# Dealing a background stream of matmul pieces to ten expert passes by their work, on one Trainium2 core

## The chip, the cores and the metric

The kernel runs on one core of a Trainium2 chip. Its time is the device time of one execution, in microseconds (us). The kernel before was run three times: 1731.17 us in the median (1726.09 to 1734.52). Names of engines: PE is TensorE (PEld its weight loads), DVE VectorE, ACT ScalarE, POOL GpSimd, SP SyncE. The queues of SP and ACT issue the loads spoken of here, on one set of 16 DMA engines.

## What is computed

Two blocks follow one another on 256 tokens of width 1024, all in float32. The first ends in a mixture of experts; the second starts with an mLSTM and pooling mixer that needs the states of a context of another 256 tokens. Cut to what matters:

```python
def first_block(x, c, ctx, ...):
    ...                                  # token mixer, residual
    x = x + gt2 * hier_moe(modulate(rms_norm(x, norm2_g), sh2, sc2), ...)
    return rms_norm(x, final_norm_g)

def hier_moe(h, wg, bg, we, be, w_gate, w_up, w_down):   # 4 groups x 8 experts, top 2
    ...                                  # router: combine[token, group, expert]
    for gi in range(N_GROUPS):
        hid = (silu(einsum('td,edf->tef', t, w_gate[gi]))
               * einsum('td,edf->tef', t, w_up[gi]) * combine[:, gi, :, None])
        out = out + einsum('tef,efd->td', hid, w_down[gi])

def mlstm_pool_mixer(hx, hc, ...):       # second block, layer 0
    uc = hc @ w_in                       # the context's half: independent of x
    hc_f, st_f = mlstm_chunkwise(...)    # 4 heads, forward and backward
    yc = mlstm_pool_output(...)          # gates, head norm, pooling, w_out
# then ctx = ctx + gate_c * rmsnorm(yc, g_post[0]), and the norm of layer 1
```

The context's half of that mixer, up to and with its two norms, does not need x. The kernel computes it while the weights of the experts arrive.

## The kernel before, in words

Each expert has three matrices of 2.1 MB. All 32 experts are loaded and used, whatever the router chose; tokens are gathered to the experts' slots by matmuls with a 0/1 matrix. The experts are done in ten passes (`PASSES`): passes 0 to 5 take four experts each (32 slots an expert), passes 6 to 9 take two (64 slots each). A pass has six steps on PE, each with one half of a matrix of each expert of the pass: gate, gate, up, up (`project`), down, down (`down`). A half is 128 x 2048 words, and the halves lie in eight slots (`half_slot`, `NHALF`). SP issues the loads of a step as soon as the step that used those slots is over (`sparse_sync`, waits on `step_used`). So in a pass of four experts two steps are loaded ahead, in a pass of two experts four. PE waits on `step_in` at the start of each step.

Between `project` and `down` a pass has on PE the gather of the next pass's tokens (`gather`), then the transposes of the hidden rows, which wait for DVE's product of both projections (`hid_out`). Behind the down projection ACT and DVE copy one half of the result each, ACT issues its store to `expert_rows` in HBM, and after the last pass POOL gathers from there the two rows of each token (`rows_pool`). ACT and DVE scale and add these at the very end of the stage, behind the rest of the context stream (`finish(body)`).

The context stream is written as generators, one each for PE, ACT and DVE (`body_pe`, `body_act`, `body_dve`), with the same number of pieces. `start(body)` takes 4 pieces; `fill(body, p, i)` takes the pieces that a table gives for pass p at place i of nine; `finish(body)` takes what is left. On PE the places 0, 1 and 2 are behind the first three halves of the projections, place 3 is behind the gather, place 4 behind the transposes, places 5 and 6 behind the two down halves, 7 and 8 at the pass's end. ACT and DVE have their places between the same dependencies. A piece on PE is mostly half of a PSUM bank's matmuls of one weight chunk: 8 matmuls 128 x 256 or 4 of 128 x 512. The pieces stand in this order: keys and values of the first two heads, gate columns, memory of head 0 and 1 (nine small pieces each, with ACT and DVE between them), output gates O and Z, queries, keys, values and memory of the other two heads, O and Z again, pool inputs PU, four pool pieces, pool gates PG, sixteen output pieces (`out_pe`, lines 1532 and 1537), and two norms of two pieces each (`norm_steps_pe`: a sum of squares, line 1253, and its spread over the partitions, line 1263). The context's weights come by ACT's queue in four slots of their own (`f_load`, line 1379), two tiles ahead.

Lines of the profile: 2346 projections, 2363 down, 2332 gather, 2379 transposes, 2218 weight loads, 1417 and 1432 pieces of context projections, 1445 and 1451 gate columns, 1462 to 1474 the start of a head's memory, 1485 to 1496 its other pieces, 2300 to 2313 the row numbers on DVE in pass 0, 2416 and 2419 ACT's copy and store, 2321 POOL's gathers, 2425 and 2476 the join of the rows, 1967 and 1973 the residual of the first norm, 424, 402 and 414 a norm of another stage with the same shapes.

Of the kernel before, what the change touches and what calls it, by code (L numbers as in the profile page):

```python
# [227 lines left out]
def build(nc, d, out):  # L228
    ctx = ExitStack()
    with ctx:  # L230
        def sb(name, shape, dt=F32):
            return ctx.enter_context(nc.sbuf_tensor(name, shape, dt))
# [27 lines left out]
        work = sb("work", [P, WORK])  # L260
# [1023 lines left out]
        NPOOL = len(POOLS)  # L1284
# [883 lines left out]
        PASSES = [(N_WIDE + 4 * i, 4) for i in range((NX - N_WIDE) // 4)] + [(2 * i, 2) for i in range(N_WIDE // 2)]  # L2168
# [50 lines left out]

        step_of = [n for n in range(6 * NPASS) for _ in range(PASSES[n // 6][1])]  # L2220

        FILL_FOUR, FILL_TWO = (2, 2, 2, 2, 2, 2, 2, 1, 1), (0, 0, 0, 1, 0, 1, 0, 0, 0)

        def fill(body, p, i):

            for _ in range((FILL_FOUR if PASSES[p][1] == 4 else FILL_TWO)[i]):
                next(body, None)

        def start(body):
# [94 lines left out]
        def sparse_pe(pe, body):  # L2324
# [12 lines left out]
            def project(p, b, n, at):  # L2337

                experts = PASSES[p][1]
                w = P // experts  # L2340
                for half in range(2):
                    pe.wait_ge(step_in[(n + half) % 4], filled_to[n + half])
                    for k in range(4 * half, 4 * half + 4):
                        for e in range(experts):
                            rows = slice(e * w, (e + 1) * w)
                            mm = nc.tensor.matmul(bank[b][rows, :], gath[:, k, rows], half_slot[(load_at[n + half] + e) % NHALF][:, (k % 4) * 512:(k % 4 + 1) * 512],  # L2346
                                                  start=(k == 0), stop=(k == DT - 1), skip_group_check=True)
                    mm.then_inc(step_used, 1)
                    if at + half < 3:
                        fill(body, p, at + half)  # L2350

            def down(p, n):

                experts = PASSES[p][1]
                w = P // experts
                for half in range(2):
                    pe.wait_ge(step_in[(n + half) % 4], filled_to[n + half])
                    for f in range(2 * half, 2 * half + 2):
                        for side in range(2):
                            for e in range(experts):  # L2360
                                rows = slice(e * w, (e + 1) * w)
                                at = (f % 2) * D + side * 512
                                mm = nc.tensor.matmul(bank[2 + side][rows, :], phid_t[:, f, rows], half_slot[(load_at[n + half] + e) % NHALF][:, at:at + 512],  # L2363
                                                      start=(f == 0), stop=(f == 3), skip_group_check=True)
                    mm.then_inc(step_used, 1)
                    fill(body, p, 5 + half)
# [3 lines left out]
            for p in range(NPASS):  # L2370
                pe.wait_ge(gath_out, 2 * p + 2)
                project(p, 0, 6 * p, 0)
                project(p, 1, 6 * p + 2, 2)
                if p < NPASS - 1:
                    gather(p + 1)
                fill(body, p, 3)
                pe.wait_ge(hid_out, p + 1)
                for f in range(4):
                    mm = nc.tensor.transpose(bank[0][:, f * P:(f + 1) * P], phid[:, f * P:(f + 1) * P], ident[:])
                mm.then_inc(phid_mm, 1)  # L2380
                fill(body, p, 4)
                if p < NPASS - 1:
                    pe.wait_ge(gath_out, 2 * p + 4)
                pe.wait_ge(phid_t_out, p + 1)
                down(p, 6 * p + 4)
                fill(body, p, 7)
                fill(body, p, 8)
# [796 lines left out]
```

## Time and profile before

| | us |
|---|---|
| median of three runs | 1731.17 |
| the profiled execution | 1726.63 |
| its span, first to last instruction | 1724.8 |
| first projection matmul of pass 0 | 540.0 |
| first of pass 6 | 995.3 |
| end of the last down projection | 1130.2 |
| last instruction of the stage (DVE) | 1166.3 |

On the page PE is busy for 90% of the span, DVE for 28%, ACT for 20%, and HBM is read at 230 GB/s on average. The 40 slices are 43 us long; slices 13 to 26 hold the expert stage, in which the DMA row reads 8 or 9 tenths and PE's 8 or 9. A busy share of an engine in a stretch is its busy time by the stretch's length. The DMA share is the mean of the 16 engines; a stretch in which they never pause reads 1.01.

### The profile page before, as it was taken

Reading aid. Unit: us, or ns where it says so; the run is one execution under the profiler, and the core shown is the slowest. Engines: PE = TensorE matmul, PEld = TensorE weight load, DVE = VectorE, ACT = ScalarE, POOL = GpSimd, SP = SyncE. Lnnn points to the kernel's source line nnn. Section 1 sums busy time; section 2 is a strip of 40 time slices with the busy share of each in tenths; the row PEclk is TensorE's granted clock in tenths of the full one; section 3 lists DMA queues with packets and bytes.
Section 4 is the critical chain, followed back from the end, with each engine's and each line's share of the span. In section 5 each row is a group of like instructions: output and inputs, shape, how many; then the busy total and the mean of one; then the engine's idle time right before and its main releaser. Section 6 shows DMA issues by size and latency. Waiting matters only on the chain.

```text
span 1724.8 us, 22009 instructions
## 1 busy us (share of the span) xinstructions
PE 1557.5 (90%) x9293; PEld 1069.7 (62%) x9293; DVE 487.9 (28%) x1221; ACT 340.9 (20%) x706; POOL 4.1 (0%) x8
## 2 busy tenths in 40 slices
PE   6999979899979879988998999976889989999997
PEld 3655678778865433643364754555676776888666
DVE  2200164451134321222114100024343322022481
ACT  2310150212021112011210000023112032021461
POOL 0000000000000000000000000000000000000000
PEclk8999996799979889999999999986999999999998
DMA  9989530122148998999999999941313223323100
GB/s 378 421 350 377 201 130 1 49 101 98 49 189 339 379 410 361 412 395 408 416 395 418 402 407 423 374 185 38 146 49 139 105 98 126 135 93 147 49 2 25
DMA packets 54303, 397.57 MB, mean 230 GB/s; under 512 B 6359, under 2 KB 13688, under 8 KB 16440
## 3 DMA queue, kind: packets, MB, share of 16 engines
q1 hardware_dynamic: 40384, 341.85, 49.4%
q10 hardware_dynamic: 13240, 52.16, 7.6%
q0 software_dynamic: 576, 2.10, 0.4%
q8 instruction: 75, 1.23, 0.3%
q14 instruction: 28, 0.23, 0.0%
HBM read 389.80 MB, written 6.29 MB: 230 GB/s over the span
## 4 chain that ended last, share of the span: by engine, by line
PE 77%; DMA 9%; DVE 5%; ACT 4%; issue 2%; SPq 1%; PEld 1%; ACTq 0%; PEldq 0%; DVEq 0%
PE bank L680 15%; PE bank L1417 12%; PE bank L1432 8%; PE bank L2346 6%; DMA work<-in_moe_w_up 4%; PE bank L2363 4%; PE bank L1532 3%; PE bank L1537 3%; PE bank L525 2%; PE bank L2332 2%; DMA work<-in_moe_w_gate 2%; PE bank L711 2%; DMA work<-in_ada_w 2%; PE bank L1140 2%; PE bank L1128 2%
## 5 line engine op out<-in xcount | busy, mean ns | idle before, releaser
L680 PE MATMUL bank<-H,ring 128*128 128x256 f32 (+1 forms) x960 | 244.7, 413 | 6.1 <-ACT work L1057 4.0
L680 PEld LDWEIGHTS bank<-H,ring 128*128 128x128 f32 x960 | 183.0, 192 | 59.7 <-issue 34.2
L2346 PE MATMUL bank<-ring,work 128*32 128x512 f32 (+1 forms) x768 | 137.4, 626 | 17.3 <-DMA work<-in_moe_w_gate 6.3
L1417 PE MATMUL bank<-H,work 128*128 128x256 f32 x512 | 114.1, 381 | 0.1
L1417 PE MATMUL bank<-H,ring 128*128 128x256 f32 x512 | 112.9, 381 | 0.0
L1417 PEld LDWEIGHTS bank<-H,work 128*128 128x128 f32 x512 | 96.0, 190 | 18.7 <-issue 6.2
L1417 PEld LDWEIGHTS bank<-H,ring 128*128 128x128 f32 x512 | 98.1, 192 | 13.6
L2346 PEld LDWEIGHTS bank<-ring,work 128*32 128x32 f32 (+1 forms) x768 | 36.5, 121 | 105.2 <-issue 83.4
L1432 PE MATMUL bank<-work,H 128*128 128x512 f32 x192 | 85.2, 596 | 0.0
L1432 PE MATMUL bank<-ring,H 128*128 128x512 f32 x192 | 83.0, 592 | 0.0
L2363 PE MATMUL bank<-ring,work 128*32 128x512 f32 (+1 forms) x384 | 67.5, 618 | 2.8 <-issue 2.2
L2346 PE MATMUL bank<-work 128*32 128x512 f32 (+1 forms) x256 | 65.4, 659 | 3.6 <-DMA work<-in_moe_w_up 3.6
L1432 PEld LDWEIGHTS bank<-work,H 128*128 128x128 f32 x192 | 35.7, 190 | 47.0 <-issue 46.9
L1432 PEld LDWEIGHTS bank<-ring,H 128*128 128x128 f32 x192 | 36.5, 190 | 44.2 <-issue 44.0
L525 PEld LDWEIGHTS bank<-work,csil 128*32 128x32 f32 x1536 | 42.5, 114 | 12.8 <-issue 11.0
L525 PE MATMUL bank<-work,csil 128*32 128x128 f32 x1536 | 49.3, 283 | 0.5 <-DMA work<-in_ada_w 0.5
L2332 PEld LDWEIGHTS bank<-work 128*128 128x128 f32 x320 | 38.1, 199 | 10.9 <-issue 7.5
L2363 PEld LDWEIGHTS bank<-ring,work 128*32 128x32 f32 (+1 forms) x384 | 18.0, 119 | 43.3 <-issue 42.4
L2332 PE MATMUL bank<-work 128*128 128x128 f32 x320 | 40.0, 285 | 3.0 <-DVE work L2440 3.0
L1485 PE MATMUL bank<-work 128*128 128x257 f32 x64 | 22.2, 430 | 18.6 <-DVE work L1799 12.9
L1496 PE MATMUL bank<-work 128*128 128x257 f32 x96 | 29.4, 415 | 9.9 <-DVEq L1816 7.8
L2469 DVE COPY work<-bank 128x512 f32<-128x512 f32 x10 | 6.9, 692 | 106.3 <-PE bank L2363 106.3
(410 smaller groups left out, 1989.3 us busy)
## 6 DMA issues: line engine op xcount, KB each, us to landing
ring<-in_moe_w_gate SPq DMA_DIRECT2D x48, 1024.0 KB, 10.4
ring<-in_moe_w_up SPq DMA_DIRECT2D x48, 1024.0 KB, 9.0
ring<-in_moe_w_down SPq DMA_DIRECT2D x48, 1024.0 KB, 11.7
work<-in_ab_w_in ACTq DMA_DIRECT2D x28, 1024.0 KB, 10.1
ring<-in_ab_w_in SPq DMA_DIRECT2D x14, 2048.0 KB, 7.5
work<-in_ada_w SPq DMA_DIRECT2D x12, 2048.0 KB, 15.6
ring<-in_w_in SPq DMA_DIRECT2D x12, 2048.0 KB, 9.6
work<-in_w_mod SPq DMA_DIRECT2D x12, 2048.0 KB, 8.9
```

The costliest lines, as they stand in the source:

```text
L525: mm = nc.tensor.matmul(bank[5][32 * g:32 * g + 32, 0:P], csil[:, m // 12, k, :], slot_k(mod_chunk[m], k, g * P, (g + 1) * P), start=(k == ...
L680: mm = nc.tensor.matmul(bank[i % NB][:, 0:n], weight(c, k, j * P, (j + 1) * P), rhs(k), start=(k == 0), stop=(k == kt - 1))
L711: mm = nc.tensor.matmul(bank[i % NB][:], H[:, k, t * P:(t + 1) * P], slot_k(c, k, 0, 512), start=(k == 0), stop=(k == DT - 1))
L1128: mm = nc.tensor.matmul(bank[4 + j % 2][:, half * T:(half + 1) * T], slot_w(c, k, j * P, (j + 1) * P), y[:, k, :], start=(k == 0), stop=(k ...
L1140: mm = nc.tensor.matmul(bank[6 + j % 2][:, 0:T], slot_k(c, k, (j % 4) * P, (j % 4 + 1) * P), mix[:, k, :], start=(k == 0), stop=(k == DT - 1))
L1417: mm = nc.tensor.matmul(b[:, j * T:(j + 1) * T], w_k(m, n, k, at, at + P), H[:, k, m.s], start=(k == 0), stop=(k == DT - 1), skip_group_ch ...
L1432: mm = nc.tensor.matmul(b[:], H[:, k, at:at + P], w_k(m, n, k, 0, 512), start=(k == 0), stop=(k == DT - 1))
L1532: nc.tensor.matmul(b[:, j * T:(j + 1) * T], w_q(m, OUT[r], 8 + k, j * P, (j + 1) * P), m.yp[:, k, :], start=(j + k == 0), stop=False, skip ...
L1537: mm = nc.tensor.matmul(b[:, j * T:(j + 1) * T], w_q(m, OUT[r], k, j * P, (j + 1) * P), m.ym[:, k, :], start=False, stop=(k == 7), skip_gr ...
L2332: mm = nc.tensor.matmul(bank[2 + k // 4][:, (k % 4) * P:(k % 4 + 1) * P], hrows[:, t, k * P:(k + 1) * P], pick[:, t, :], start=(t == 0), s ...
L2346: mm = nc.tensor.matmul(bank[b][rows, :], gath[:, k, rows], half_slot[(load_at[n + half] + e) % NHALF][:, (k % 4) * 512:(k % 4 + 1) * 512] ...
L2363: mm = nc.tensor.matmul(bank[2 + side][rows, :], phid_t[:, f, rows], half_slot[(load_at[n + half] + e) % NHALF][:, at:at + 512], start=(f ...
```

## The change

The two tables `FILL_FOUR` and `FILL_TWO`, which gave every pass of four experts 15 pieces and every pass of two experts 2, are replaced by a table worked out from the pieces' work. `BODY` lists what each piece is reckoned to cost (8 for a full one, down to 0), `PASS_SHARE` says how much of it a pass gets (85 for four experts, 36 for two, none for the last), and `spread` deals the pieces in their order. The last pass gets the four norm pieces by a row of its own. Nothing else differs; the pieces, their order and all loads are the same.

```diff
-        FILL_FOUR, FILL_TWO = (2, 2, 2, 2, 2, 2, 2, 1, 1), (0, 0, 0, 1, 0, 1, 0, 0, 0)
+        TILE, LIGHT = 8, 2
+        MEMORY = (5,) + (1, 2) * 2 + (3, 2) * 2
+        HEADS_OUT = MEMORY * 2 + (TILE,) * 8 + (LIGHT,)
+        BODY = ((TILE,) * 4 + (LIGHT,) + HEADS_OUT + (TILE,) * 12 + HEADS_OUT + (TILE,) * 8 + (0,) + (4,) * NPOOL + (TILE,) * 8 + (TILE,) * 16)
+        SHARE = (1, 1, 1, 1, 1, 1, 1, 0.5, 0.5)
+        PASS_SHARE = [85 if experts == 4 else 36 for _, experts in PASSES[:-1]]
+        NORM_TURNS = (0, 1, 1, 0, 1, 1, 0, 0, 0)
+        def spread(work):
+            table, at, spent, due = [], 0, 0.0, 0.0
+            for share in PASS_SHARE:
+                row = []
+                for part in SHARE:
+                    due += share * part / sum(SHARE)
+                    n = 0
+                    while at < len(work) and spent + work[at] / 2 <= due:
+                        spent += work[at]
+                        at += 1
+                        n += 1
+                    row.append(n)
+                table.append(tuple(row))
+            return table
+        FILL = spread(BODY) + [NORM_TURNS]
 ...
         def fill(body, p, i):
-            for _ in range((FILL_FOUR if PASSES[p][1] == 4 else FILL_TWO)[i]):
+            for _ in range(FILL[p][i]):
                 next(body, None)
```

Worked out, the new table has these rows, one a pass; behind each the units of `BODY` that the pass gets, and those that it got from the old table:

```
pass 0  (1, 2, 1, 5, 4, 5, 4, 1, 1)   84 units, before  61
pass 1  (1, 2, 1, 1, 2, 2, 1, 1, 1)   90 units, before  81
pass 2  (1, 1, 1, 2, 1, 1, 3, 3, 2)   80 units, before 105
pass 3  (4, 5, 3, 1, 2, 1, 1, 1, 1)   90 units, before  49
pass 4  (2, 1, 1, 2, 1, 1, 3, 1, 2)   82 units, before 114
pass 5  (1, 2, 1, 1, 2, 1, 1, 1, 1)   88 units, before 112
pass 6  (0, 1, 0, 1, 0, 1, 0, 1, 0)   32 units, before  16
pass 7  (1, 0, 1, 0, 1, 0, 1, 0, 1)   40 units, before  16
pass 8  (0, 1, 0, 1, 0, 1, 0, 1, 0)   32 units, before  16
pass 9  (0, 1, 1, 0, 1, 1, 0, 0, 0)    0 units, before  16
left for finish                        0 units, before  32
```

On PE, the last pass before: L2346 are projection halves, L2363 down halves, L1532 and L1537 output pieces, L1253 and L1263 the norms' sums and spreads.

```order
L2346 MATMUL bank<-ring,work 64x512 x16
L1537 MATMUL bank<-H,work 128x256 x8
L2379 MATMUL bank<-ident,work 128x128 x4
L2363 MATMUL bank<-ring,work 64x512 x8
L1537 MATMUL bank<-H,work 128x256 x8
L2363 MATMUL bank<-work 64x512 x8
L1532 MATMUL bank<-work 128x256 x16
L1537 MATMUL bank<-H,work 128x256 x16
L1253 MATMUL bank<-H,ones 32x64 x32
L1263 MATMUL bank<-rstd,ident 128x64 x4
L1253 MATMUL bank<-H,ones 32x64 x32
L1263 MATMUL bank<-rstd,ident 128x64 x4
```

And now, from its second projection half on (projections are L2371, down halves L2388, transposes L2404 in the changed file):

```order
L2371 MATMUL bank<-work 64x512 x8
L1253 MATMUL bank<-H,ones 32x64 x32
L2371 MATMUL bank<-ring,work 64x512 x8
L1263 MATMUL bank<-rstd,ident 128x64 x4
L2371 MATMUL bank<-ring,work 64x512 x8
L2404 MATMUL bank<-ident,work 128x128 x4
L1253 MATMUL bank<-H,ones 32x64 x32
L2388 MATMUL bank<-ring,work 64x512 x8
L1263 MATMUL bank<-rstd,ident 128x64 x4
L2388 MATMUL bank<-work 64x512 x8
L2284 UNCONDITIONAL_BRANCH
```

The output pieces have left the last pass and the stretch behind it, the norms stand among its steps, and the last down half is the last thing that PE does in the stage.

On PE in pass 8 before, from its first projection half to its last down half:

```order
L2346 MATMUL bank<-ring,work 64x512 x24
L2346 MATMUL bank<-work 64x512 x8
L2332 MATMUL bank<-work 128x128 x16
L1532 MATMUL bank<-work 128x256 x8
L2379 MATMUL bank<-ident,work 128x128 x4
L2363 MATMUL bank<-ring,work 64x512 x8
L1532 MATMUL bank<-work 128x256 x8
L2363 MATMUL bank<-ring,work 64x512 x8
```

And now:

```order
L2371 MATMUL bank<-ring,work 64x512 x16
L1532 MATMUL bank<-work 128x256 x8
L2371 MATMUL bank<-ring,work 64x512 x8
L2371 MATMUL bank<-work 64x512 x8
L2357 MATMUL bank<-work 128x128 x16
L1532 MATMUL bank<-work 128x256 x8
L2404 MATMUL bank<-ident,work 128x128 x4
L2388 MATMUL bank<-ring,work 64x512 x8
L1537 MATMUL bank<-H,work 128x256 x8
L2388 MATMUL bank<-ring,work 64x512 x8
L1537 MATMUL bank<-H,work 128x256 x8
```

Four output pieces stand in the pass, where two stood.

On PE in pass 0 before, behind its fourth projection half (L2332 is the gather, L1485 and L1496 are memory pieces of head 0):

```order
L2332 MATMUL bank<-work 128x128 x16
L1485 MATMUL bank<-work 128x257
L1496 MATMUL bank<-work 128x257 x2
L2379 MATMUL bank<-ident,work 128x128 x4
L1485 MATMUL bank<-work 128x257
L1496 MATMUL bank<-work 128x257 x2
L2363 MATMUL bank<-ring,work 32x512 x16
```

And now (L1445 to L1474 are the gate columns and the head's start):

```order
L1445 MATMUL bank<-ident,work 128x64 x8
L1451 MATMUL bank<-work,ident 128x2 x8
L1462 MATMUL bank<-work,ident 128x256 x2
L1469 MATMUL bank<-work 128x128 x4
L1474 MATMUL bank<-ident,work 128x128 x4
L1485 MATMUL bank<-work 128x257
L1496 MATMUL bank<-work 128x257 x2
L1485 MATMUL bank<-work 128x257
L2404 MATMUL bank<-ident,work 128x128 x4
L1496 MATMUL bank<-work 128x257 x2
L1485 MATMUL bank<-work 128x257
L1490 MATMUL bank<-work 128x257 x2
```

The gate columns and the start of the head, which stood between the third and the fourth projection half, have moved behind the fourth, together with more memory pieces than before.

## Rows read from the trace of the kernel before

**Rows 1.** Stretches: length, busy PE, PEld, DVE, ACT, POOL, then PEclk, DMA share, GB/s.
```profile
540.00:995.30 455.30, 410.56 (x2275) 223.36 (x2276) 107.66 (x258) 66.69 (x125) 0.00 (x0) 0.96 0.98 399
995.30:1130.20 134.90, 128.49 (x624) 64.16 (x624) 7.57 (x12) 11.49 (x20) 0.00 (x0) 0.97 0.97 398
1130.20:1166.30 36.10, 22.19 (x210) 17.60 (x208) 13.68 (x32) 12.21 (x24) 3.90 (x4) 0.76 0.38 133
```

**Rows 2.** The same view, pass 0, then passes 6 to 9.
```profile
540.00:611.80 71.80, 62.05 (x351) 30.37 (x350) 24.20 (x74) 15.12 (x32) 0.00 (x0) 0.90 0.94 383
...
995.30:1028.50 33.20, 32.48 (x166) 16.98 (x168) 1.71 (x3) 2.85 (x6) 0.00 (x0) 1.00 1.01 423
1028.50:1061.50 33.00, 32.28 (x166) 16.91 (x164) 2.40 (x4) 3.43 (x6) 0.00 (x0) 1.00 0.99 402
1061.50:1100.70 39.20, 34.91 (x164) 17.28 (x162) 2.07 (x3) 2.36 (x4) 0.00 (x0) 0.91 0.95 390
1100.70:1130.20 29.50, 28.82 (x134) 12.99 (x130) 1.38 (x2) 2.85 (x5) 0.00 (x0) 1.00 0.92 374
```

**Rows 3.** Timeline of PE, passes 6 and 8 (start us, us, operation, idle before).
```profile
1005.55 3.60 PE L2346 MATMUL bank<-work 128*64 128x512 f32 x16
...
1012.76 3.63 PE L1532 MATMUL bank<-work 128*128 128x256 f32 x16
...
1017.55 3.65 PE L2363 MATMUL bank<-ring,work 128*64 128x512 f32 x16 [0.72 <-issue]
...
1075.33 6.27 PE L2346 MATMUL bank<-work 128*64 128x512 f32 x16 [3.57 <-DMA work<-in_moe_w_up]
```

**Rows 4.** Timeline of PE, passes 0 and 3; then busy time from 580 to 600.
```profile
565.28 0.71 PE L1445 MATMUL bank<-ident,work 64*128 64x64 f32 x8 [0.40 <-ACT work L1593]
...
570.50 1.06 PE L1474 MATMUL bank<-ident,work 128*128 128x128 f32 x4
...
575.67 3.84 PE L2332 MATMUL bank<-work 128*128 128x128 f32 x32
579.35 0.60 PE L1485 MATMUL bank<-work 128*128 128x257 f32 x2
...
582.72 0.67 PE L1496 MATMUL bank<-work 128*128 128x257 f32 x2
587.43 1.23 PE L1496 MATMUL bank<-work 128*128 128x257 f32 x2 [4.04 <-DVEq L1816]
...
762.75 0.77 PE L1485 MATMUL bank<-work 128*128 128x257 f32 x2 [2.21 <-DVE work L1799]
...
580.00:600.00 20.00, 14.55 (x80) 5.65 (x82) 10.12 (x39) 1.06 (x2) 0.00 (x0) 0.83 0.82 328
```

**Rows 5.** Timeline behind the last down half, all engines; then busy time there.
```profile
1131.16 0.33 ACTq L2419 DMA_DIRECT2D expert_rows<-work  x1
1140.68 1.08 POOL L2321 DMA_INDIRECT work<-expert_rows,work  x1 [1140.22 <-DMA expert_rows<-work]
...
1148.97 0.87 DVE L1967 SCALAR_TENSOR_TENSOR work<-work,gcoef,bank 128x256 f32<-128x256 f32 x2 [1.25 <-PE bank L1263]
...
1154.12 0.76 DVE L1973 TENSOR_TENSOR X<-X,work 128x256 f32<-128x256 f32 x2
...
1162.65 2.18 ACT L2425 ACTIVATE work<-work 128x1024 f32<-128x1024 f32 x2
...
1172.25 2.56 ACT L424 ACTIVATE H<-X 128x256 f32<-128x256 f32 x8 [7.42 <-DVE X L2752]
1172.72 2.59 PE L402 MATMUL bank<-H,ones 128*32 128x64 f32 x64 [1.08 <-ACT H L424]
...
1176.33 1.97 PE L414 MATMUL bank<-rstd,ident 128*128 128x64 f32 x8 [1.02 <-DVE rstd L435]
...
1145.00:1150.00 5.00, 1.99 (x34) 1.44 (x28) 1.60 (x5) 2.09 (x4) 0.49 (x1) 0.89 0.80 288
1150.00:1155.00 5.00, 2.64 (x48) 1.23 (x48) 4.97 (x16) 2.93 (x8) 0.00 (x0) 0.50 0.00 0
```

More of the change, by code:

```diff
@@ L2220, in build @@
         step_of = [n for n in range(6 * NPASS) for _ in range(PASSES[n // 6][1])]
-        FILL_FOUR, FILL_TWO = (2, 2, 2, 2, 2, 2, 2, 1, 1), (0, 0, 0, 1, 0, 1, 0, 0, 0)
+        TILE, LIGHT = 8, 2
[20 more added lines that the diff above has]
+        FILL = spread(BODY) + [NORM_TURNS]
+        assert sum(map(sum, FILL)) == len(BODY) + 4
         def fill(body, p, i):
-            for _ in range((FILL_FOUR if PASSES[p][1] == 4 else FILL_TWO)[i]):
+            for _ in range(FILL[p][i]):
                 next(body, None)
```

## The prediction, on record before the changed kernel ran

> **What bounds the kernel now.** I read the page first, its slices and its chain of waits, then cut the expert stage into three stretches [rows 1]. From 540.0 to 995.3 us run the six passes of four experts, from there to 1130.2 the four passes of two experts, and from 1130.2 to 1166.3 what is left behind the last down projection. The reader is to see two engines at their limit together: in the first two stretches PE is busy 410.56 of 455.3 us and 128.49 of 134.9, and the DMA share is 0.98 and 0.97, where a full stretch reads 1.01 [rows 2]. In the third PE has 22.19 of 36.1 us and the DMA share is 0.38. So moving PE work forward out of the third stretch pays only where PE is waiting, and the question is whether PE waits where the change puts it.
>
> By pass [rows 2]: passes 6 and 7 take 33.2 and 33.0 us with 32.48 and 32.28 busy. Their one idle piece is 0.72 us before the first down half [rows 3]. Pass 8 takes 39.2 because PE waits 3.57 us for a weight and then needs 6.27 us for matmuls that take 3.60 elsewhere [rows 3]. A two-expert pass is therefore a PE stretch: the expert's own matmuls and two output pieces of 3.6 us each [rows 3]. Its weights arrive about as fast (share 1.01, 0.99), but they would not if PE were slower.
>
> **Stretch one, 455.3 us.** In the units of the new table (8 is one piece of 3.6 us) the old one deals 61, 81, 105, 49, 114, 112 to passes 0 to 5, 522 together; the new one 84, 90, 80, 90, 82, 88, 514 together. PE work falls by one piece, 3.6 us, which hardly matters, since weights set the pace of most of it. What an even deal can recover is the time in which DMA was not full: (1.01 - 0.98) x 455.3 = 13.7 us [rows 1, 2]. Against that stands pass 0. Behind the fourth projection half there now come, without a weight in between, the gather (3.8 us), the gate columns with the head's start (565.28 to 571.56, 6.3 us), a wait for that head's scores (2.2 us, as the next head shows), three memory pieces of about 1.0 us, the transposes, the 4.04 us in which DVE works out the row numbers, and four more pieces: 3.8 + 6.3 + 2.2 + 3.0 + 0.4 + 4.0 + 4.5 = 24.2 us [rows 4], and the first down half behind it, 3.6 to 5.6. Only two bundles of four halves are then in flight. A half is 128 x 2048 words, 1.05 MB, so eight are 8.4 MB, 20 us at the 423 GB/s of pass 6 [rows 2], and two context loads 5 us; the first bundle is asked for when the third half ends, at 564.9, which is 10.8 us before the fourth half ends at 575.7 [rows 4]. So DMA has work until about 590, the first down half ends about 24.2 + 3.6 behind 575.7, at 603.5 to 605.5, and DMA is dry for some 13 us. Before, the same place shows a share of 0.82 in the 20 us from 580 to 600, 3.8 us lost [rows 4]. The hole grows by about 9 us, and of the 13.7 us about 10 lie elsewhere and can be got back. The ends are -14 (every gap closed, no hole) and +13 (the hole and nothing recovered, and memory pieces at their latency). I take +2, near what the two make together, with a little kept back because nothing recovers fully.
>
> **Stretch two, 134.9 us.** Output pieces in passes 6 to 9: old 2, 2, 2, 2; new 4, 5, 4, 0. That is 13 for 8, 5 x 3.6 = +18.0 us on an engine with no idle time to give but pass 8's. That goes, since weights now have 40 us instead of 33 for each pass: -(3.57 + 6.27 - 3.60) = -6.2 us. The last pass carries four norm pieces in place of two output pieces, already counted out. Priced by such pieces [rows 5], where PE has nothing else: the first sum of squares 2.6; its spread 2.0; then DVE scales and adds 16 operations from 1148.97 to 1154.88, 5.9 us, while PE has one projection half of 3.6, and DVE's product of the hidden rows, 0.7, is queued behind them, so PE waits 3.0; the second sum must follow eight squares on ACT that start behind its copy of the transposed rows, 0.6 for the copy, 2.6 for the squares and 0.5 for the last matmuls, less the 0.7 that PE waits there now, 3.0; the second spread 2.0. Together 12.6 us. Its ends are 7 (two sums, and two spreads at the doubled clock, 2 x (2.6 + 1.0), all else hidden) and 18 (each of the two waits is followed by matmuls slowed by 2.7 us, as pass 8's was). So the stretch becomes 134.9 + 18.0 - 6.2 + 12.6 = 159.3 us, +24.4.
>
> **Stretch three, 36.1 us.** Now 14.2 us of output pieces, then the norms to 1162.65, then ACT and DVE join the experts' rows, 3.65 us to 1166.30 [rows 5]. With PE's tail gone, what is late next is the rows' own way: from the last down half 1.0 us to the store's issue at 1131.16; the store until POOL issues the first of four gathers, 1140.68; and DMA falls silent between 1149 and 1150 (share 0.80 of 1145 to 1150, 0.00 after) [rows 5]. That is 19.3 us from 1130.2, hidden before, and bare now. 19.3 + 3.65 = 23.0 us, a gain of 13.1. Its ends are 20 and 26: the store shares DMA with a 2 MB load for the next stage as it did before. ACT may have to change its table once.
>
> **Sum.** +2 + 24.4 - 13.1 = +13.3 us. The profiled execution took 1726.63 us (span 1724.8); it becomes 1739.9. The three runs' median is 4.5 above it, 1731.17, so by the median 1744.5. All later stages are unchanged.
>
> **Rivals.**
> *The stream fills up.* Every PE piece that leaves the tail goes under a weight wait. Then only the weights count, and the stage ends 13.1 us sooner or more. For it: the DMA shares of 0.98 and 0.97, and the 44.7 us in which PE is idle in stretch one [rows 1]. Against it: passes 6 and 7 have no such idle time, and 56 more units, 25 us, go into passes 6 to 8. It gives 1731.2 - 13 = 1718. The Trainium skill speaks for this one: "Perfetto Trace Analysis", Optimization Strategy, says that where the most contended engine changes over time, interleaving the regimes may improve performance, and an expert stream beside a PE-only tail is such a pair. By that rule the sum would be the third stretch's -13.1 and nothing in the second; the trace agrees for passes of four experts, where PE is idle 45 of 455 us, and not for those of two, idle 0.7 of 33.
> *A draw.* The 13.7 us of stretch one are all recovered and pass 0's hole is small: -12 + 24.4 - 13.1, about -1: 1730.5.
> *Pass 0's hole persists and the clock falls.* Where PE now waits for each bundle it also runs slower behind the wait: +13 in the first stretch, norms at 18, the rows' way at 26: +13 + 29.8 - 10.1 = +32.7: 1764. It decides from the point where waits pass two microseconds: one of 3.57 us had its matmuls at 6.27 [rows 3]. The Trainium skill, "TensorE: Matmul & The Clock Gate", HAM oscillation, says that a loop which waits for DMA between short bursts runs each burst at half clock. By it every bundle of the first stretch would cost PE 2 us more, but under a DMA wait, so the sum stays unless weights stop being last.
> *The change doesn't do what it says.* The stream could still end behind the last pass. The order of PE leaves no piece behind the last down half, so this has no chance of its own.
>
> **How the numbers follow.** Forecast, +5 to +24: 0.60. Stream fills up, below -9: 0.07. Draw, -9 to +5: 0.20. Persisting hole, over +24: 0.13. A median of this kernel can tell about 0.5%, 8.7 us, from no change. The forecast's lower part, +5 to +8.7, about 0.07 of chance, falls within that. So faster 0.07, same 0.27, slower 0.66. The range from 1728 to 1761 leaves out the first rival and the worst of the last. The forecast's own range is 1736 to 1755.
>
> **What would show it.** Right: passes 6, 7 and 8 at about 40, 44 and 40 us, with a DMA share near 0.8 and no weight wait; pass 9 at 35; 23 us from the last down half to the end of the stage; a DMA share near 0.6 somewhere in 590 to 605. Wrong: pass 6 starting before 985 (the draw), weight waits in passes 6 to 8, norm pieces with no waits on ACT or DVE, or rows landing within 15 us.

## Result and profile after

The changed kernel took 1768.91 us in the median (1767.20 to 1774.71, 4 runs), the kernel before 1730.01 on the same chip: ratio 1.0238, 95% interval 1.0213 to 1.0262 (the ratio is estimated from all runs; the two medians alone give 1.0225). It is slower, as forecast, but by 2.4% where 0.8% (13.3 us) was forecast, and outside the range. The profiled execution took 1768.1 us (span 1766.3).

The three stretches of the changed kernel (columns as in rows 1):

```profile
540.88:1027.03 486.15, 413.86 (x2258) 220.26 (x2260) 107.23 (x258) 66.60 (x125) 0.00 (x0) 0.93 0.91 368
1027.03:1184.55 157.52, 151.90 (x848) 82.39 (x848) 17.98 (x41) 19.95 (x41) 0.00 (x0) 0.98 0.89 358
1184.55:1207.90 23.35, 0.00 (x0) 0.00 (x0) 3.17 (x3) 2.92 (x4) 3.88 (x4) 0.56 0.59 204
```

Against [rows 1] that is +30.9, +22.6 and -12.8 us, 40.7 of the 41.5 us by which the span grew. The forecast was +2, +24.4 and -13.1. The whole miss is in stretch one: 30.9 us longer at 3.3 us more busy time on PE, with the DMA share down from 0.98 to 0.91. Passes 1 to 5 have 8.5 us of it (391.9 instead of 383.4) and pass 0 has 22.4.

By pass (same view; passes 0, 1, 3 and 5 to 9; passes 2 and 4 have shares of 0.99 and 1.00):

```profile
540.80:635.00 94.20, 75.73 (x389) 38.07 (x388) 32.97 (x102) 16.55 (x34) 0.00 (x0) 0.89 0.77 312
635.00:710.20 75.20, 67.60 (x357) 33.04 (x357) 10.14 (x21) 13.64 (x23) 0.00 (x0) 0.95 0.92 372
...
793.80:867.80 74.00, 67.72 (x355) 30.61 (x355) 18.51 (x49) 15.31 (x31) 0.00 (x0) 1.00 0.87 342
...
949.80:1027.00 77.20, 67.47 (x407) 42.92 (x406) 6.05 (x10) 4.75 (x8) 0.00 (x0) 0.92 0.91 371
1027.00:1067.60 40.60, 39.88 (x198) 22.58 (x198) 2.40 (x4) 3.43 (x6) 0.00 (x0) 1.00 1.01 422
1067.60:1110.90 43.30, 43.30 (x215) 25.38 (x214) 2.40 (x4) 3.43 (x6) 0.00 (x0) 1.00 0.94 381
1110.90:1151.50 40.60, 39.88 (x197) 22.61 (x196) 2.07 (x3) 3.43 (x6) 0.00 (x0) 1.00 0.79 307
1151.50:1184.50 33.00, 28.84 (x245) 11.85 (x244) 11.10 (x30) 9.61 (x23) 0.00 (x0) 0.90 0.79 314
```

Call dry time what DMA lacks to its full share, (1.01 - share) x length. Pass 0 has 0.24 x 94.2 = 22.6 us of it; before, 0.07 x 71.8 = 5.0 [rows 2]. Pass 0 alone is 22.4 us longer than before. Passes 1 to 5 have 27.3 us of dry time (10.4 of it in pass 3, 7.7 in pass 5, 6.8 in pass 1), and before, from the same view, 11.6. Dry time grew by 33 us, the stretch by 31. That the two agree is bookkeeping: the loads are the same, so whatever makes the stretch longer is added to its dry time. Dry time says where the time went; what caused it needs the rows below and the experiments.

What pass 0 does shows on PE, behind the fourth projection half (the place that rows 4 show of the kernel before; start, us, operation, idle before):

```profile
574.78 3.84 PE L2357 MATMUL bank<-work 128*128 128x128 f32 x32
580.00 0.72 PE L1445 MATMUL bank<-ident,work 64*128 64x64 f32 x8 [1.38 <-ACT work L1593]
...
588.14 0.67 PE L1485 MATMUL bank<-work 128*128 128x257 f32 x2 [1.70 <-issue]
...
591.90 1.06 PE L2404 MATMUL bank<-ident,work 128*128 128x128 f32 x4
...
598.37 1.20 PE L1485 MATMUL bank<-work 128*128 128x257 f32 x2 [3.69 <-DVEq L1840]
...
605.61 3.64 PE L2388 MATMUL bank<-ring,work 128*32 128x512 f32 x32
...
615.23 0.67 PE L1485 MATMUL bank<-work 128*128 128x257 f32 x2 [2.06 <-DVE work L1799]
...
618.95 0.62 PE L2388 MATMUL bank<-ring,work 128*32 128x512 f32 x2
```

and on SP's queue, which can ask for four more weight halves (a bundle) only when a step on PE has used its own four. Each pair of rows is two bundles, eight loads: the first four are issued at the start of the pair, the other four at its end. First the kernel before, then the changed one (start of the first issue, time from the first to the last of the row):

```profile
564.94 11.67 SPq L2218 DMA_DIRECT2D ring<-in_moe_w_down  x6
576.71 0.85 SPq L2218 DMA_DIRECT2D work<-in_moe_w_down  x2
594.37 7.76 SPq L2218 DMA_DIRECT2D ring<-in_moe_w_gate  x6
602.32 0.85 SPq L2218 DMA_DIRECT2D work<-in_moe_w_gate  x2
615.53 10.28 SPq L2218 DMA_DIRECT2D ring<-in_moe_w_up  x6
```

```profile
562.35 13.39 SPq L2218 DMA_DIRECT2D ring<-in_moe_w_down  x6
575.83 0.85 SPq L2218 DMA_DIRECT2D work<-in_moe_w_down  x2
609.46 14.18 SPq L2218 DMA_DIRECT2D ring<-in_moe_w_gate  x6
623.82 1.09 SPq L2218 DMA_DIRECT2D work<-in_moe_w_gate  x2
638.76 8.01 SPq L2218 DMA_DIRECT2D ring<-in_moe_w_up  x6
```

The reader is to see one silence grow from 594.37 - 577.56 = 16.8 to 609.46 - 576.68 = 32.8 us, between the end of the fourth step and the end of the fifth. DMA still has work for some 15.6 us of it: it is full up to 590 and busy for 2.3 us of the next ten. Over the whole of pass 0's second half, the way from the group for `down` to that for `up` takes 76.4 us instead of 50.6. DMA in and behind the silence:

```profile
580.00:590.00 10.00, 8.15 (x46) 6.46 (x46) 2.88 (x11) 2.85 (x8) 0.00 (x0) 0.83 1.01 419
590.00:600.00 10.00, 5.49 (x15) 3.97 (x15) 6.79 (x27) 0.59 (x1) 0.00 (x0) 0.50 0.23 97
600.00:610.00 10.00, 9.22 (x49) 4.31 (x48) 3.74 (x13) 0.95 (x2) 0.00 (x0) 0.82 0.01 2
620.00:640.00 20.00, 17.31 (x94) 7.80 (x84) 6.50 (x19) 2.82 (x4) 0.00 (x0) 1.00 0.72 264
```

PE then waits for weights (waits of PE from 540 to 1210; total, times, longest), where the longest such wait before was 4.1 us:

```profile
PE bank L2371 <- DMA work<-in_moe_w_up: 26.2, 5, 9.7
...
PE bank L2371 <- DMA work<-in_moe_w_gate: 11.6, 2, 6.1
PE bank L1485 <- DVEq L1840: 9.0, 10, 3.7
```

Weight waits on PE are 40.1 us in all, 20.9 before. They stand in passes 1, 2, 4 and 5 too, the longest (9.7 us) at 985.65, so not all of them can be put down to pass 0.

The last pass, and then what follows it, which rows 5 show of the kernel before:

```profile
1158.54 1.10 PE L1253 MATMUL bank<-H,ones 128*32 128x64 f32 x64
...
1170.93 1.11 PE L2404 MATMUL bank<-ident,work 128*128 128x128 f32 x4 [3.08 <-DVE work L2477]
1173.12 2.49 PE L1253 MATMUL bank<-H,ones 128*32 128x64 f32 x64 [1.08 <-ACT H L1698]
1175.54 4.38 PE L2388 MATMUL bank<-ring,work 128*64 128x512 f32 x16
```

```profile
1185.43 0.33 ACTq L2444 DMA_DIRECT2D expert_rows<-work  x1
1194.87 1.07 POOL L2346 DMA_INDIRECT work<-expert_rows,work  x1 [1194.41 <-DMA expert_rows<-work]
...
1204.24 2.19 ACT L2450 ACTIVATE work<-work 128x1024 f32<-128x1024 f32 x2 [18.96 <-DMA work<-expert_rows,work]
```

### The profile page after: what moved, and what is told of

It is laid out like the page before. It is cut to its first block, busy times and chain, and to the rows that moved or that the text cites. A ratio compares the mean times of both kernels' runs of the same rounds, so it can differ in the third digit from the quotient of the medians.

```text
span 1766.3 us, 22009 instructions
## 1 busy us (share of the span) xinstructions
PE 1563.6 (89%) x9293; PEld 1068.5 (60%) x9293; DVE 487.2 (28%) x1221; ACT 339.7 (19%) x706; POOL 4.1 (0%) x8
## 4 chain that ended last, share of the span: by engine, by line
PE 75%; DMA 10%; DVE 6%; ACT 4%; issue 2%; SPq 1%; PEld 1%; ACTq 0%; PEldq 0%; DVEq 0%; POOL 0%; POOLq 0%
PE bank L680 14%; PE bank L1417 10%; PE bank L1432 8%; PE bank L2371 7%; DMA work<-in_moe_w_up 5%; PE bank L2388 4%; PE bank L1537 3%; PE bank L1532 3%; DMA work<-in_moe_w_gate 3%; PE bank L525 2%; PE bank L2357 2%; PE bank L711 2%; DMA work<-in_ada_w 2%; PE bank L1140 2%; PE bank L1128 2%
## 5 line engine op out<-in xcount | busy, mean ns | idle before, releaser
L2371 PE MATMUL bank<-ring,work 128*32 128x512 f32 (+1 forms) x768 | 142.6, 633 | 40.1 <-DMA work<-in_moe_w_up 26.2
L2371 PEld LDWEIGHTS bank<-ring,work 128*32 128x32 f32 (+1 forms) x768 | 36.2, 122 | 130.9 <-issue 84.7
L1417 PEld LDWEIGHTS bank<-H,ring 128*128 128x128 f32 x512 | 98.2, 192 | 13.7
L2371 PE MATMUL bank<-work 128*32 128x512 f32 (+1 forms) x256 | 69.1, 689 | 0.0
L2388 PE MATMUL bank<-ring,work 128*32 128x512 f32 (+1 forms) x384 | 66.3, 600 | 1.4 <-issue 1.4
L2477 DVE TENSOR_TENSOR work<-work,bank 128x512 f32<-128x512 f32 x10 | 6.9, 688 | 180.5 <-PE bank L2371 180.5
L1485 PE MATMUL bank<-work 128*128 128x257 f32 x64 | 23.7, 455 | 30.2 <-DVE work L1799 17.8
L525 PEld LDWEIGHTS bank<-work,csil 128*32 128x32 f32 x1536 | 42.7, 114 | 12.5 <-issue 11.0
L2388 PEld LDWEIGHTS bank<-ring,work 128*32 128x32 f32 (+1 forms) x384 | 17.6, 117 | 41.2 <-issue 41.2
L1496 PE MATMUL bank<-work 128*128 128x257 f32 x96 | 31.7, 436 | 7.2 <-DVEq L1816 4.6
```

Source lines behind the costliest of these rows:

```text
L525: mm = nc.tensor.matmul(bank[5][32 * g:32 * g + 32, 0:P], csil[:, m // 12, k, :], slot_k(mod_chunk[m], k, g * P, (g + 1) * P), start=(k == ...
L1417: mm = nc.tensor.matmul(b[:, j * T:(j + 1) * T], w_k(m, n, k, at, at + P), H[:, k, m.s], start=(k == 0), stop=(k == DT - 1), skip_group_ch ...
```

## The experiments

All keep the order of the stream and all loads; only the table or the reckoned costs differ. `O` stands for `(2, 2, 2, 2, 2, 2, 2, 1, 1)`, the row of before. That row deals 16 pieces; the "15" in the text above the prediction is a slip, its units are right. Lengths are from each kernel's one profile; ratios are to the kernel before on the same chip, from 4 to 12 runs of each. The last column tells how far the profiled run lies from its kernel's median: lengths of two kernels that differ by less than this are not told apart.

| kernel | ratio (95%) | pass 0 | stretch one | two | end | profile less median |
|---|---|---|---|---|---|---|
| before | 1 | 71.9 | 455.2 | 135.1 | 36.0 | -3.4 |
| changed | 1.0238 (1.0213-1.0262) | 94.2 | 486.2 | 157.6 | 23.3 | -0.8 |
| old_head_new_tail | 1.0056 (1.0036-1.0075) | 72.0 | 454.4 | 155.0 | 23.4 | -3.4 |
| new_head_old_tail | 1.0224 (1.0199-1.0250) | 97.7 | 493.1 | 137.7 | 39.4 | +5.0 |
| tail_norms_only | 0.9997 (0.9970-1.0023) | 71.6 | 458.0 | 144.5 | 23.9 | +3.3 |
| memory_by_time | 1.0116 (1.0085-1.0147) | 81.6 | 473.5 | 156.5 | 23.3 | +0.7 |
| even_gaps | 1.0103 (1.0071-1.0135) | 82.1 | 473.7 | 159.9 | 23.4 | +13.5 |
| even_time | 1.0102 (1.0069-1.0136) | 77.1 | 459.1 | 160.2 | 23.7 | -6.0 |
| even_time_tail | 1.0021 (0.9997-1.0046) | 77.8 | 462.3 | 144.5 | 24.5 | +0.1 |
| even_time_more | 0.9985 (0.9964-1.0005) | 78.0 | 469.3 | 130.9 | 24.4 | +2.2 |
| old_pass_zero | 1.0087 (1.0063-1.0112) | 72.2 | 458.9 | 157.6 | 23.3 | -4.7 |
| old_plus_two | 1.0054 (1.0033-1.0075) | 72.9 | 474.8 | 139.8 | 24.7 | +2.9 |
| old_plus_four | 1.0027 (1.0003-1.0052) | 71.7 | 471.9 | 128.7 | 24.4 | -5.0 |
| old_plus_six | 0.9912 (0.9892-0.9931) | 74.5 | 474.6 | 123.8 | 24.2 | +6.4 |

**Which half of the table costs.**

```diff
-        FILL = spread(BODY) + [NORM_TURNS]
+        FILL = [O] * 6 + [(0, 1, 0, 1, 0, 1, 0, 1, 0)] * 3 + [NORM_TURNS]      # old_head_new_tail
+        FILL = spread(BODY)[:6] + [(0, 0, 0, 1, 0, 1, 0, 0, 0)] * 4            # new_head_old_tail
+        FILL = [O] * 6 + [(0, 1, 0, 1, 0, 1, 0, 0, 0)] * 4                     # tail_norms_only
```

> Passes 0 to 5 are dealt as before the change (16 pieces each), passes 6 to 8 four output pieces each, pass 9 the two norms. If the loss sits in the six passes of four experts: stretch one back at 455 us, stretch two 134.9 + 4 x 3.6 - 6.2 + 10.6 (what the norms cost in the changed kernel's last pass, 32.9 against 29.5 less two pieces) = 153.7, the way behind the last down half 23.4; in sum 6 us slower than before (about 0.4%). If the loss sits in what the later passes and the last one carry: 30 us or more slower, as the changed kernel.

> Passes 0 to 5 are dealt as in the changed kernel, passes 6 to 9 two output pieces each as before, and five output pieces and the norms are left behind the last pass. If the loss sits in the six passes of four experts: stretch one 486, stretch two 128.7 (no weight wait), behind the last down half 39.7; 28 us slower than before (1.6%). If it sits in the later passes: within 5 us of before.

> Passes 0 to 5 as before the change, passes 6 to 9 three output pieces each, the two norms left behind the last pass. If the rows' way over HBM (23 us) is the floor behind the last down half and hides two norms (18.4 us) fully, then stretch two is 134.9 + 4 x 3.6 - 6.2 = 143.1, the rest 23.4, and the kernel is 4.5 us faster than before (0.3%); the norms in the last pass were then worth nothing. If norms behind the last pass cost their own time beside the rows' way: 36.1 - 14.2 = 21.9 plus some waits, up to 30 us, and 2 us slower than before.

With the old six rows stretch one is 454.4 us again; with the new six rows and the old tail it is 493.1. The excess belongs to the six rows alone. The tail's part is a trade of some +20 for -12.5 us in the profile, and the kernel with the old head comes out at +0.56%. The third kernel splits that: three output pieces in each two-expert pass and the norms left at the end. Its stretch two is 10.5 us shorter than old_head_new_tail's and its end only 0.4 longer. Why shows behind its last down half, all engines (L1704 is the last operation of the norms):

```profile
1148.18 0.33 ACTq L2444 DMA_DIRECT2D expert_rows<-work  x1
...
1157.97 1.07 POOL L2346 DMA_INDIRECT work<-expert_rows,work  x1 [1157.51 <-DMA expert_rows<-work]
...
1163.32 3.30 ACT L1704 ACTIVATE H<-H,mod 128x256 f32<-128x256 f32 x8 [3.23 <-DVE H L1984]
1167.51 2.19 ACT L2450 ACTIVATE work<-work 128x1024 f32<-128x1024 f32 x2 [0.88 <-DMA work<-expert_rows,work]
```

The norms end at 1166.62, inside the 19.3 us between the store's issue and ACT's work on the landed rows. Moving them into the last pass pays 10 us to empty a stretch that gets only 0.4 us shorter by it.

**What in the six rows costs.** Two theories: the memory pieces are reckoned at their PE work, though a packed head waits on ACT and DVE between its pieces (nine pieces, 21 units or 9.4 us of PE work, were reckoned to take 18.6 us back to back); or the table crowds PE between the fourth and fifth half, where only two bundles are in flight.

```diff
-        MEMORY = (5,) + (1, 2) * 2 + (3, 2) * 2
+        MEMORY = (11, 4, 3, 3, 3, 5, 5, 5, 4)          # memory_by_time; pass share 85 -> 100
-        SHARE = (1, 1, 1, 1, 1, 1, 1, 0.5, 0.5)
+        SHARE = (1.5, 1.5, 1.5, 0.25, 0.25, 1.5, 0.75, 0.375, 0.375)          # even_gaps
+        # even_time: both edits, pool pieces (9,) * NPOOL, pass share 103
```

> The changed kernel with each head's nine memory pieces reckoned at their measured time back to back (43 units, 18.6 us, for 21) and the share of a pass of four experts raised from 85 to 100 to match. Theory one (memory pieces are reckoned at half their time, so passes 0 and 3 get too much PE time between weights): pass 0 falls from 94 to about 76 us, stretch one from 486 to 460 to 465, the kernel is 20 to 25 us faster than the changed one, 15 us slower than before. Theory two (an equal deal keeps PE waiting for each bundle, and two bundles, 20 us of loads, do not cover the long way between the fourth and the fifth half of every pass): stretch one stays at 475 or more, and each pass still shows its DMA gap there.

> The changed kernel with its reckoned prices kept, but within a pass places 3 and 4 (between the fourth and the fifth half, where the gather and the transposes stand anyway) get a sixth of their share and places 0, 1, 2 and 5 half as much again. Theory two (with weights just arriving, the 20 us of loads in flight must cover two PE stretches; the one between the fourth and fifth half is too long): the DMA gaps at that place in passes 1, 2, 3 and 5, 3 to 4 us each, go, pass 0's hole of 22 us shrinks too, stretch one 486 to about 468, the kernel 15 to 20 us faster than the changed one. Theory one alone (only the memory pieces' price matters): within 5 us of the changed kernel, since they are packed as before.

> Both at once: places 3 and 4 nearly empty and memory pieces (and pool pieces, 9 units for 4) at their measured time. If the two theories together hold all of the loss in stretch one, the DMA share there is 1.00 and stretch one takes 442 to 450 us; with stretch two 157 and the end 23.3 the kernel is 5 to 12 us slower than before, 30 us faster than the changed one. If something else keeps DMA from being full: stretch one at 465 or more, 22 us slower than before.

In the profiles each alone takes about 12.6 us off stretch one, both together 27.1 of the 30.9. And each acts in pass 0 (pass 0 of the first two; same columns):

```profile
538.20:619.80 81.60, 67.11 (x365) 33.25 (x368) 27.35 (x86) 14.21 (x31) 0.00 (x0) 0.87 0.83 337
```

```profile
544.50:626.60 82.10, 74.24 (x391) 38.16 (x391) 32.82 (x102) 16.57 (x34) 0.00 (x0) 0.90 0.84 337
```

Passes 1 to 5 together take 391.9 us in the changed kernel and 391.9 and 391.5 in these two. On SP's queue the two edits close different silences: the group for `down` to that for `gate` to that for `up` takes 47.1 and 29.3 us in the changed kernel, 42.6 and 21.1 in memory_by_time, 30.3 and 30.6 in even_gaps, 23.7 and 20.9 in even_time (29.4 and 21.2 before). That the two causes add up is seen in the profiles only, and is not shown. By the ratios each edit alone takes 1.2 to 1.3% off the changed kernel and both together no more than one; even_gaps' profiled run was its slowest, and even_time's median stands 6 us above its own profile. What is shown is that either edit gives back about half of the loss, and that theory one alone falls: by it even_gaps was to stay within 5 us of the changed kernel, and it is 20 us faster. memory_by_time parts the theories less well, since it deals all six rows anew and takes five pieces out of pass 0 (19 for 24).

**Pass 0 by itself.**

```diff
-        PASS_SHARE = [85 if experts == 4 else 36 for _, experts in PASSES[:-1]]
-        FILL = spread(BODY) + [NORM_TURNS]
+        PASS_SHARE = [90] * 5
+        FILL = [O] + spread(BODY[16:]) + TWOS + [NORM_TURNS]    # TWOS: the change's rows 6 to 8
```

> The changed kernel with pass 0 alone dealt as before (16 pieces, 61 units instead of 84); the rest of the stream is spread over passes 1 to 5 by the same rule, 90 units each, and passes 6 to 9 are those of the change. Pass 0 was 94.2 us in the changed kernel, 71.9 before, and its DMA was dry for 22.6 us against 5. Theory: the gap belongs to the pass whose row is crowded between the fourth and the fifth half, and is not made up later. Pass 0 is back at 72 us; pass 1 begins with eight memory pieces of the second head at its places 0 and 1, where two bundles are in flight, and may pay some 5 us for them; stretch one 486.2 - 17.6 + 5 = about 472 us (466 to 478), the kernel some 12 us faster than the changed one, near 1755. Rival: the stretch is what its total of pieces and weights makes of it, and a hole closed in one pass opens in another: stretch one 483 or more, within 0.3% of the changed kernel.

Pass 0 has its old row, and the rule of the change deals what is left, so passes 1 to 5 have even rows too, but not those of the changed kernel (17, 12, 23, 15 and 12 pieces for 12, 15, 19, 14 and 11). Stretch one is 27.3 us shorter in the profile, and the ratio 1.0238 becomes 1.0087: 26 us of the kernel's time, or 22 by the medians. So even dealing of five passes is nearly free, and the loss came with the row that the rule gave to pass 0. The new row of pass 0 beside the old rows of the others was not tried. Passes 0, 1 and 3 (same view):

```profile
538.70:610.90 72.20, 61.96 (x355) 30.47 (x354) 24.18 (x74) 14.44 (x31) 0.00 (x0) 0.91 0.94 383
610.90:685.60 74.70, 68.25 (x351) 31.52 (x351) 16.07 (x43) 14.00 (x24) 0.00 (x0) 0.98 1.00 406
...
763.50:837.60 74.10, 67.02 (x361) 31.27 (x360) 23.22 (x65) 17.14 (x35) 0.00 (x0) 1.00 0.91 372
```

The hole does not come back elsewhere: pass 1, which now begins with eight memory pieces packed into two places, reads 1.00. The rival of a total that closes itself falls. The theory, which had 17.6 us come back and 5 lost again, was too small. Passes 1 to 5 take 386.7 us here and 391.9 in the changed kernel. Whether those 5 us were pass 0's hole handed on to later passes stays open: their rows differ, and in memory_by_time and even_gaps passes 1 to 5 got no shorter though pass 0 did.

**Versions meant to be faster.**

```diff
+        FILL = spread(BODY)[:6] + [(0, 1, 0, 1, 0, 1, 0, 0, 0)] * 4     # even_time_tail, pass share 105
+        FILL = spread(BODY)[:6] + [(0, 1, 0, 0, 0, 1, 0, 0, 0)] * 4     # even_time_more, share 110.5
+        # before's table; passes 1 and 3 get one more piece at place 0 (two), at 0 and 1 (four),
+        # at 0, 1 and 2 (six); passes 6 to 9 get 3, 3, 2, 2 pieces (two), 2, 2, 2, 2 (four), 2, 2, 1, 1 (six)
```

> The same deal in passes 0 to 5, but passes 6 to 9 take three output pieces each and the norms stay behind the last pass, where the rows' way hides them. Stretch one as in even_time (442 to 450), stretch two 144.5 and the end 23.9 as measured with that tail: 10 to 15 us faster than before (0.6 to 0.9%). If PE lacks the time in passes 6 to 9 because it starts them without weights in stock: up to 6 us of that is lost.

> As even_time_tail, with eight output pieces dealt to passes 0 to 5 in place of four and two to each of passes 6 to 9. If PE still has time to spare in stretch one (44.7 us idle before the change, 12 more would be used for 14.4 of pieces), stretch one stays at 442 to 452, stretch two falls to 129 to 135, and the kernel is 15 to 25 us faster than before. If PE is at its limit there once the deal is even: stretch one grows by the 14.4 us that stretch two loses, and it runs as even_time_tail.

> The old deal with one piece more at place 0 of passes 1 and 3, in which PE waits for weights in the kernel before (4.3 and 4.1 us for the first of them), so six output pieces fall to passes 0 to 5; passes 6 and 7 take three, passes 8 and 9 two, and the norms stay behind the last pass. If PE's idle time in passes 1 and 3 is free for pieces: stretch one 455 to 459, stretch two 134.9 - 6.2 + 2 x 3.6 = 136, end 24.4: 8 to 11 us faster than before (0.5 to 0.6%). If every piece more in stretch one costs its 3.6 us there: as tail_norms_only, no change.

> As old_plus_two, with three pieces at places 0, 1 and 2 of passes 1 and 3, ten output pieces in passes 0 to 5, two each in passes 6 and 7 and one each in passes 8 and 9. If PE's idle time in passes 1 and 3 (10.6 and 11.6 us) is free for pieces: stretch one 457 to 462, stretch two 122 to 128 (weights become last there, 31 us a pass and more), end 24.4: 10 to 18 us faster than before. If a third piece between two halves makes DMA run dry as in the changed kernel: stretch one 470 or more and no gain.

> The table before with one more piece at places 0 and 1 of passes 1 and 3, all else as before: the four output pieces that stood behind the last pass are drawn into the stretch of the six passes. It stands between the kernel with two more pieces there (stretch one 474.8 us, 19.6 more than before) and the one with six (474.6). Theory one, the price is that of the shift (memory pieces and transposes of the stream fall on other places, DMA has gaps of some 15 us in all), once, whatever the number: stretch one 474 to 476, stretch two 131 to 135, the end 24.3, so +19.5 - 2 - 11.7 = about +6 us against before, 1735. Theory two, the price is 3.6 us of PE a piece or less, and two more pieces were an unlucky hit: stretch one 464 to 470, and -3 us or better against before, 1726 or less.

Each has its stream but for the norms out before the last down half, and the norms behind it. The first two were put 10 to 15 and 15 to 25 us below the kernel before and came out level with it: their stretch one took 462.3 and 469.3 us, not 442 to 450 and 442 to 452. old_plus_two was put 8 to 11 us faster and is 0.54% slower. old_plus_six beats both kernels: 1716.47 us in the median, by the ratio 0.88% less than before. Its three stretches:

```profile
539.14:1013.77 474.63, 433.73 (x2369) 242.80 (x2369) 107.50 (x258) 67.59 (x128) 0.00 (x0) 0.95 0.96 391
1013.77:1137.55 123.78, 118.43 (x597) 58.76 (x600) 7.57 (x12) 10.30 (x18) 0.00 (x0) 1.00 0.98 397
1137.55:1161.74 24.19, 7.53 (x144) 5.25 (x144) 13.63 (x32) 11.23 (x22) 3.88 (x4) 0.60 0.63 227
```

In the profile six pieces more cost 19.4 us in the first stretch, two fewer in the second save 11.3, and the end saves 11.8, only 3.7 us in all; the profiled run was the slowest of six. The gain came otherwise than expected: by the expectation stretch one was to take 457 to 462 us, or 470 and more with no gain, and it took 474.6 with a gain.

With two, four and six pieces more stretch one is 474.8, 471.9 and 474.6 us. At 3.6 us a piece it would be 462, 470 and 477, so what stands out is old_plus_two. Four was to tell a price paid once (474 to 476 us, +6) from two more pieces having been an unlucky hit (464 to 470, -3 or better); it measured 471.9 and +0.27%, nearer the first, but in neither span. The profiled runs lie 2.9 above, 5.0 below and 6.4 above their medians, as much as the three lengths differ. By the ratios old_plus_six is 1.4% or 24 us faster than old_plus_two, of which stretch two and the end show 16.5, so six may cost less than two. The extra pieces move every later memory piece and transpose to another place, and DMA has gaps that before's table had not: in old_plus_two passes 2 and 4 read a share of 0.91 and 0.94 (0.98 and 0.99 before), and weight waits on PE are 28.9 us (20.9 before). Which of the shifted pieces does it stays open, and so does the price of a piece.

## Why the prediction was wrong

Its failed step is "Stretch one, 455.3 us": "The hole grows by about 9 us, and of the 13.7 us about 10 lie elsewhere and can be got back ... I take +2". Measured +30.9, beyond its own end of +13: pass 0 grew by 22.4 us where 9 was reckoned, and passes 1 to 5 grew by 8.5 where 10 was to come back.

- The place and the mechanism were right: DMA ran dry in pass 0, between the fourth step and the end of the fifth, because nothing could be asked for.
- The way on PE was too short. From the fourth step to the first down half 24.2 us were reckoned, and the half was to end at 603.5 to 605.5. It began at 605.61, 30.8 us behind the start of the gather at 574.78, and the next loads were asked for behind its end, at 609.46. The sum left out the 1.38 us for which the gate columns wait for ACT. And from 588.14 on, the memory pieces and the transposes took 13.8 us beside the wait of 3.69, where 7.9 were reckoned: the granted clock read 0.50 from 590 to 600 and 0.82 in the ten us behind it, and short waits stand between them.
- So the hole was 17.8 us and not 13: from 590 to 610 the dry time is (1.01 - 0.23) x 10 + (1.01 - 0.01) x 10. The sign "a DMA share near 0.6 somewhere in 590 to 605" didn't even fit the prediction's own 13 us; it read 0.23 and then 0.01.
- The second silence was not in the sum. Behind the fifth half stand the rest of head 0 and the start of head 1, again with ACT and DVE in between, and the sixth half begins only at 618.95. From 620 to 640 that is 0.29 x 20 = 5.8 us dry. In memory_by_time, which thins out the heads, this second interval is back at 21.1 us.
- "About 10 lie elsewhere and can be got back": nothing was. With pass 0's old row and five even ones (old_pass_zero) passes 1 to 5 take 386.7 us, still 3.3 more than the uneven rows of before. Why even rows recover nothing there, no run shows.

With pass 0 mended stretch one is 458.9 us, +3.6, about the +2 of the sum, and the ratio of 1.0087 is 15 us, beside the forecast's 13.3. That is partly luck: the hole of 9 and the recovery of 10 in the sum are both absent from that kernel, and its profiled run lies 4.7 us below its median.

The other two terms held. Stretch two was forecast at 159.3 us and took 157.5: passes 6, 7 and 8 at "about 40, 44 and 40" took 40.6, 43.3 and 40.6, without a weight wait. The DMA share "near 0.8" came only in pass 8; they read 1.01, 0.94 and 0.79. Pass 8 got its wait back (39.2 us with two pieces before, 40.6 with four now) as said. Pass 9 was forecast at 35 and took 33.0. Of its norm terms the 3.0 us wait behind DVE is there (3.08), the second sum waits 1.08 and not 3.0, and the first sum takes 1.10 and not 2.6: the same 64 matmuls took 2.49 behind a wait of 3.08 and one of 1.08. Stretch three was 23.0 forecast and 23.35 measured, each step of it: store issued 0.9 us behind the last half, 9.4 us until POOL, 9.4 more until ACT.

The rivals. "The stream fills up" fell where it was said to: interleaving gained 12.8 us at the end and cost 22.6 in passes in which PE had next to no idle time, before the 30.9. The Trainium skill, "Perfetto Trace Analysis", Optimization Strategy, says that performance may be improved by interleaving such regimes; here it was not. "A draw" fell with the 13.7 us that could not be recovered. "Pass 0's hole persists and the clock falls", 0.13, was nearest in time, 1764, but for other reasons: it had the norms at 18 us (10.7) and the rows' way at 26 (23.35), and its +13 in stretch one was less than half. The clock fell little: 0.93 against 0.96 over the stretch.

What the prediction had not considered at all is that the norms at the end were free. "With PE's tail gone, what is late next is the rows' own way" names the cover, and the next question, what may stay under it, was not asked. It would have shown the change's last row, 10.7 us in pass 9, as a pure loss (tail_norms_only: 10.5 us shorter stretch two, 0.4 longer end).

## What to carry to other kernels

Before work is spread evenly under a stream of loads, look at when each load can be *asked for*: the longest stretch between the ends of two consumers must be shorter than the loads that are still under way when it starts. Two bundles are 20 us of loads, but the first of them has partly landed by then. Here DMA had work for 15.6 us; a stretch of 16.8 us already cost 3.8, and one of 32.8 cost 17.8. Small pieces that wait on other engines count by their time in the trace, not by their matmuls. When a tail is emptied, find what bounds it next, and leave under it all that fits. Test a table row by row: here the old row in one pass, with even rows in the other five, took back 22 to 26 us of 39 to 41. And look at how far each profiled run lies from its kernel's median before lengths of stretches are compared.

## What the runs showed of the hardware

- A wait's length alone did not say whether the matmuls after it ran at half speed. Half a projection took 3.64 us after waits of 1.98 and 2.41 us, but 5.34 after 2.20 and 6.58 after 2.38. Timeline of PE, the kernel before and then old_plus_two:

```profile
629.96 5.34 PE L2346 MATMUL bank<-ring,work 128*32 128x512 f32 x32 [2.20 <-DMA ring<-in_moe_w_up]
...
787.26 3.64 PE L2346 MATMUL bank<-ring,work 128*32 128x512 f32 x32 [1.98 <-DMA ring<-in_moe_w_up]
```

```profile
630.80 6.58 PE L2371 MATMUL bank<-ring,work 128*32 128x512 f32 x32 [2.38 <-DMA ring<-in_moe_w_up]
...
794.63 3.64 PE L2371 MATMUL bank<-ring,work 128*32 128x512 f32 x32 [2.41 <-DMA ring<-in_moe_w_up]
```

All four are projection halves in passes of four experts. Over the four halves the granted clock read 0.68, 1.00, 0.55 and 1.00. The prediction's "point where waits pass two microseconds" fits the kernel before (1.98 us and then full speed, 2.15 and 2.20 and then slowed) but not old_plus_two; what else decides was not tried.

- Dry time of DMA was not made up later: no pass of any kernel read a share above 1.02 or more than 425 GB/s (pass 9 of old_plus_six; pass 6 of the changed kernel 1.01 and 422), and stretch one, with 33 us more of dry time, was 31 us longer.
- The store of the last expert rows took 9.0 us to land (issued 1185.43, landed 1194.41), and from POOL's first gather to ACT were another 9.4 (1194.87 to 1204.24). In the eleven other kernels whose output pieces were out before the last down half the end lay between 23.3 and 24.7 us too, with or without norms in it.
